# Four convolved feature chunks moved from the memory stage to the sample stage, and the decay sums of the SSD branch loaded from DRAM instead of multiplied on TensorE

## What is computed

```
h = _rmsnorm(x, norm_in_w)
u = h @ w_in
z_ssd, xbc, dt_raw, qkv, z_att, q_mem, z_mem, gate_raw = _split_in(u)
y_ssd = _ssd_branch(z_ssd, xbc, dt_raw, ...)    # conv(4)+SiLU on xbc, chunked scan, gated norm
outs, lses = dilated attention, 3 groups x 8 heads (sample queries read the caches)
y_att = merged outs * silu(z_att)
y_mem = _mem_attn(q_mem, mem_kv) * silu(z_mem)
merged = sum over branches of gate * (y_branch @ w_br)
y = _rmsnorm(x + merged @ w_out, norm_f_w)
```

```
acs = cumsum(dt * a_neg)                        # over the chunk's 128 tokens
lmat = exp(where(tril, acs[l] - acs[s], -inf))
y_diag = ((C B^T) * lmat) @ (x * dt)
```

## Time and profile before

| | us |
|---|---|
| median of 3 runs | 2171.91 |
| lowest and highest run | 2169.57, 2172.75 |
| profiled execution | 2172.42 |
| its span | 2170.6 |
| busy PE / DVE / ACT / POOL | 2029.3 / 990.8 / 755.5 / 237.5 |
| memory stage, 182 to 401 | 219.0, PE busy 219.0 |
| sample stage and set-up, 1092 to 1499 | 407.0, PE busy 377.3 |
| SSD core up to its seventh chunk, 1499 to 1764 | 265.0, PE busy 247.3 |

### The profile page before, as it was taken

One profiled execution on the slowest core, in us unless ns is written; L12 is line 12 of the kernel. 1 busy time (PEld: TensorE's weight loads), 2 busy tenths in 40 slices (PEclk: granted clock), 3 DMA queues, 4 the chain that ended last, 5 costly groups with the idle time before them and its releaser, 6 DMA issues.

```text
span 2170.6 us, 35280 instructions
## 1 busy us (share of the span) xinstructions
PE 2029.3 (93%) x14555; PEld 1929.4 (89%) x14555; DVE 990.8 (46%) x1948; ACT 755.5 (35%) x1635; POOL 237.5 (11%) x358
## 2 busy tenths in 40 slices
PE   5999999999989999999999789999999979969997
PEld 5899999999889999999999679759999969969997
DVE  5214676525454445343346871103444465454423
ACT  5223354223443323233645112305364553132202
POOL 1000112100001011112123000001111111100000
PEclk9999999999999999999999888999999989989998
DMA  6211233211112121212266665483333545554422
GB/s 211 88 42 60 80 91 90 82 46 51 37 32 66 38 66 47 77 63 67 87 196 193 209 209 161 165 297 110 108 117 101 163 145 179 166 183 136 137 82 104
DMA packets 166992, 248.76 MB, mean 115 GB/s; under 512 B 19701, under 2 KB 114613, under 8 KB 166805
## 3 DMA queue, kind: packets, MB, share of 16 engines
q1 hardware_dynamic: 144576, 179.51, 26.5%
q0 software_dynamic: 22256, 66.98, 9.1%
HBM read 179.74 MB, written 66.70 MB: 114 GB/s over the span
## 4 chain that ended last, share of the span: by engine, by line
PE 75%; DVE 9%; ACT 6%; DMA 5%; issue 4%; SPq 0%; DVEq 0%; POOL 0%; ACTq 0%; POOLq 0%
PE bank L2236 19%; PE bank L2237 18%; PE bank L2238 18%; PE bank L2432 2%; DMA acc<-acc_T 2%; PE bank L2407 2%; DVE w_lo L1698 2%; PE bank L2538 1%; PE bank L2390 1%; PE bank L2648 1%; PE bank L2368 1%; ACT soft L1512 1%; DVE softT L1950 1%; PE bank L2471 1%; ACT Lm L1625 1%
## 5 line engine op out<-in xcount | busy, mean ns | idle before, releaser
L2236 PE MATMUL bank<-w_hi,hT_hi 128*128 128x256 f32 (+1 forms) x1848 | 534.5, 289 | 3.4 <-DVE hT_lo L2106 3.4
L2237 PE MATMUL bank<-w_lo,hT_hi 128*128 128x256 f32 (+1 forms) x1848 | 522.7, 283 | 0.0
L2238 PE MATMUL bank<-w_hi,hT_lo 128*128 128x256 f32 (+1 forms) x1848 | 521.9, 282 | 0.0
L2236 PE MATMUL bank<-hT_hi,w_hi 128*128 128x352 f32 x1344 | 458.3, 341 | 6.3 <-DVE acc L2083 5.7
L2238 PE MATMUL bank<-hT_hi,w_lo 128*128 128x352 f32 x1344 | 444.7, 331 | 0.0
L2237 PE MATMUL bank<-hT_lo,w_hi 128*128 128x352 f32 x1344 | 444.4, 331 | 0.0
L2236 PEld LDWEIGHTS bank<-w_hi,hT_hi 128*128 128x128 f32 (+1 forms) x1848 | 347.5, 188 | 4.9 <-issue 3.6
L2238 PEld LDWEIGHTS bank<-w_hi,hT_lo 128*128 128x128 f32 (+1 forms) x1848 | 348.6, 189 | 0.6
L2237 PEld LDWEIGHTS bank<-w_lo,hT_hi 128*128 128x128 f32 (+1 forms) x1848 | 347.6, 188 | 0.7
L2236 PEld LDWEIGHTS bank<-hT_hi,w_hi 128*128 128x128 f32 x1344 | 263.6, 196 | 16.7 <-issue 7.5
L2237 PEld LDWEIGHTS bank<-hT_lo,w_hi 128*128 128x128 f32 x1344 | 264.1, 197 | 1.1
(11 more groups left out here) (417 smaller groups left out, 2993.9 us busy)
## 6 DMA issues: line engine op xcount, KB each, us to landing
w_raw<-in_w_in SPq DMA_DIRECT2D x96, 512.0 KB, 4.9
kvring<-in_cache_win_kv SPq DMA_DIRECT2D x120, 256.0 KB, 3.6
feat_T<-fstage POOLq DMA_DIRECT2D x40, 528.0 KB, 3.8
fstage<-feat_T SPq DMA_DIRECT2D x16, 528.0 KB, 4.4
xc<-feat_T SPq DMA_DIRECT2D x8, 1024.0 KB, 5.8
kvring<-in_cache_mem_kv SPq DMA_DIRECT2D x28, 256.0 KB, 3.8
o_rows<-obuf POOLq DMA_DIRECT2D x48, 132.0 KB, 2.0
mo<-o_rows SPq DMA_DIRECT2D x24, 264.0 KB, 3.9
```

The costliest lines, as they stand in the source:

```text
L2236: pe.matmul(out, xh(k), wh(k), start=(k == 0), stop=False)
L2237: pe.matmul(out, xh(k), wl(k), start=False, stop=False)
L2238: ins = pe.matmul(out, xl(k), wh(k), start=False, stop=(k == nk - 1))
```

## The change

**Part 1, the chunks.** `N_MEM_FILL` is 4: four of the eight convolved chunks move from the memory stage to the sample stage, behind the first two gate chunks, where they become chunks 38 to 41. The sample stage gets its fillers by part: 3 chunks beside the merges, 3.5 beside the 64 scored-on-DVE key sets, 1 beside the 24 turned ones, 1.5 beside the softmax, 3 beside the value sets; 12 where there were 9. A thirteenth follows beside the set-up, and the core holds 7 where it held 6. Value sets stand in groups of 4, not 8. The late convolved chunks all use `fraw_a`, are written in up to five pieces, and wait for the convolution of the feature before. SP waits for the store of the last convolved feature ahead of the first `xc`. A `low` never overtakes another.

**Part 2, the decay sums.** The 128 D products of the prompt's chunks (c below 8) are gone. One matmul in `ssd_dA` gives the running sums of all chunks and heads transposed (row = chunk and head, column = token); DVE copies them to `yraw`, SP writes them to DRAM (`sum_T`, 64 KB) and waits until they are there, then loads them back four rows at a time, broadcast over the 128 partitions (256 KB), into two slots `sums`: 32 loads, load i waiting for the relus of load i - 2. ACT's relu reads `sums` in SBUF in place of PSUM. The loads share the semaphores of the key and value loads.

```diff
-N_MEM_FILL, N_TAIL_FILL, N_SAMPLE_FILL = 8, 2, 9
+N_MEM_FILL, N_TAIL_FILL = 4, 2
+FILL_MERGE, FILL_KEYS, FILL_TURNED, FILL_SOFT, FILL_VALUES = 3, 3.5, 1, 1.5, 3
...
+    fill_src = conv[:N_MEM_FILL] + [("za", i, "w_in", C_ZATT + CW * i) for i in range(2)]
     fill_src += [("z", i, "w_in", C_Z + CW * i) for i in range(4)]
+    fill_src += gates[:2] + conv[N_MEM_FILL:] + gates[2:]
...
-    side += [sum(sval[i:i + 8], []) for i in range(0, len(sval), 8)]
-    sched += spread(side, steps)
+    parts.append(([sum(sval[i:i + 4], []) for i in range(0, len(sval), 4)], FILL_VALUES))
+    steps = gate_steps(round(sum(fill for _, fill in parts)))
...
+        while at < len(sched) and sched[at][0] == "low":
+            at += 1
...
+            def load_sums(i):
+
+                if i >= NSUM:
+                    sp.wait_ge(s_ddf, i - NSUM + 1)
+                sp.dma_start(sums[:, i % NSUM, :, :].rearrange("p h l -> p (h l)"),
+                             sumT[4 * i:4 * i + 4, :].rearrange("h l -> (h l)").partition_broadcast(P)).then_inc(sum_landed(i)[0], 16)
...
                     if c == 0:
                         late_free(sp)
+                        conv_stored(sp)
...
+                elif s[0] == "ssd_dA":
+                    late_free(sp)
+                    sp.wait_ge(s_s0, 4)
+                    first, count = value_sem(NRING), value_landed(len(values) - 1 - (len(values) - 1 - NRING) % NVAL)
+                    sp.dma_start(sumT, yraw[:, 0:P]).then_inc(first, 16)
+                    sp.wait_ge(first, count + 16)
+                    for i in range(NSUM):
+                        load_sums(i)
+                elif s[0] == "ssd" and s[2] in (1, 2) and s[1] < NB:
+                    for i in range(4 * s[1] + 2 * s[2] - 2 + NSUM, 4 * s[1] + 2 * s[2] + NSUM):
+                        if i < 4 * NB:
+                            load_sums(i)
...
-                            if c >= 2:
+                            if c > 2 * N_MEM_FILL:
+                                act.wait_ge(s_conv, c)
+                                act.wait_ge(s_tail[(c - 1) % 2], 32 * ((c + 1) // 2))
+                            elif c >= 2:
...
-                            act.wait_ge(s_dD, 4 * c + qq + 1)
+                            if c < NB:
+                                act.wait_ge(*sum_landed(4 * c + qq))
+                                later = sums[:, (4 * c + qq) % NSUM, :, :]
...
+                    dve.tensor_copy(yraw[:, 0:P], bank[7][:, P:2 * P])
...
+                    pe.matmul(bank[7][:, P:2 * P], dA[:, 0:P], table("upper"), start=True, stop=True)
...
-                    elif q in (1, 2):
-                        up = (table("upper") if c < NB else table("upper_s"))[0:m, 0:m]
+                    elif q in (1, 2) and c == NB:
+                        up = table("upper_s")[0:m, 0:m]
...
-                            pe.wait_ge(s_ddf, 4 * c + 8)
+                            pe.wait_ge(s_dxt, c + 2)
```

More of the change, by code:

```diff
@@ L272, in plan @@
     side += [[("sprep", 0)], [], [("sscore", 0)], []]
[L273 to L280 removed]
+    parts = [(side, FILL_MERGE)]
+    n_prod = 2 * TS * BS
+    for lo, hi, fill in ((0, n_prod, FILL_KEYS), (n_prod, len(sets) + 1, FILL_TURNED)):
+        parts.append(([[("skey", n) for n in range(i, min(i + 4, hi))] for i in range(lo, hi, 4)], fill))
+    parts.append(([[("ssoft", 0)], [], [], [("ssoft", 1)], [], [], [("ssoft", 2)], [], []], FILL_SOFT))
     sval = []
@@ L285, in plan @@
         sval[-1] += [("soT", y) for y in range(4) if part_end[y] + 5 == n]
-    side += [sum(sval[i:i + 8], []) for i in range(0, len(sval), 8)]
-    sched += spread(side, steps)
+    parts.append(([sum(sval[i:i + 4], []) for i in range(0, len(sval), 4)], FILL_VALUES))
+    steps = gate_steps(round(sum(fill for _, fill in parts)))
+    done, upto = 0, 0
+    for part, fill in parts:
+        upto += fill
+        last = round(len(steps) * upto / sum(f for _, f in parts))
+        sched += spread(part, steps[done:last])
+        done = last
     steps = gate_steps(1)
@@ L561, in build_program @@
         yraw = sb(area, "yraw", [P, TOK])
+        last = ExitStack()
+        sums = sb(last, "sums", [P, NSUM, 4, P])
+        last.close()
         yst2 = sb(area, "yst2", [P, KT8, NS])
@@ L919, in value_landed, with sum_landed @@
             return 16 * (n // NVAL + 1 + (key_loads((len(sets) + r) % NRING) if r < NRING else 0))
+        def sum_landed(i):
+            x = 3 + i % NSUM
+            return s_kv[x], 16 * (key_loads(x) + len(range((x - len(sets)) % NRING, len(values), NVAL)) + i // NSUM + 1)
         def probs_turned(eng, half):
@@ L1007, in wait_part1_stores, with conv_stored @@
                 eng.wait_ge(s_tail[i], 16 * 16)
+        def conv_stored(eng):
+            last = max(feat_no[x] for x in conv_no)
+            for i in range(2):
+                eng.wait_ge(s_fst[i], 16 * ((last + 2 - i) // 2))
+                eng.wait_ge(s_tail[i], 16 * 16)
         def gates_stored(eng):
```

38 lines of the change are left out of this document (20 added, 18 removed).

## The result

| | median us | lowest to highest | runs |
|---|---|---|---|
| before | 2172.33 | 2169.57 to 2176.25 | 4 |
| changed | 2217.88 | 2215.75 to 2219.12 | 4 |

A forecast was written before the change was run, and what follows sets the result against it. PE, busy 93% of the span, was taken as the bound. Memory stage -73, sample stage +19 and core +15 gave -39 us from 2172.4, so 2133 us; range 2107 to 2162, faster 0.87.

The forecast's parts named there:

- so -22: SSD core: removing the D products frees 16 x 1.87 = 30 us of PE, less the last two chunks, hence -22 us.
- 83 to 95: Value sets in the sample stage: PE work and transfers near equal, 83 to 95 us.
- Memory stage: Memory units: four chunks leave for -92.8 us, stalls give back 17 and lower clock 3, net -73 us.
- Merges, key sets, turned sets: Sample stage: merges 105 to 83 us, key sets 96 to 104, turned sets 63 to 74, softmax 31 to 42.
- Start: Start of the core: first transpose waits for `xc` behind the sums' write and loads, +13 us, between +4 and +20.
- Rival C: Value sets bound by transfers at 217 GB/s, 124 us in place of 95, whole 2162 us; chance 9%.
- go too: -5: SSD core: PE's waits for ACT's release of the D banks beside filler, 5.0 us, vanish: -5 us.
- Rival E: Core: D products were hidden in waits for DVE, removing them gains nothing, core +30 us, whole 2148; chance 8%.
- The split of chunk 50, +6: Core: this split waits on ACT for weights loaded after the previous `w_lo`, once on the path: +6 us, between 0 and 12.
- Rule on the relu: Core: skill's fixed costs make each SBUF relu 43 ns longer, 5.5 us of ACT, sum at most 1 us higher.
- rival D: Core: sums come late in every chunk, ACT waits some 3 us each, PE behind it: +18 us, 2151; chance 12%.

The follow-up runs named there:

- Part 2 alone: Only the loaded decay sums replacing D products, plan and fillers as before, against the kernel before: 2206.81 us, ratio 1.0174.
- part 1 alone: Only the chunks moved as in the change, D still multiplied on TensorE, no loads of sums, against the kernel before: 2195.57 us, ratio 1.0129.
- with the products back, unused: Kernel with only the loaded sums, but PE again makes the 128 D products, which nothing reads: 2192.44 us, ratio 1.0099 against the kernel before.

## Why the prediction was wrong

The forecast was 82 us off: -39 against a span 43 us longer. Two terms failed, the D products of the core ("so -22", and -5 with them) and the values ("83 to 95"); each of the others was within 9 us.

**Memory stage: right,** -71.5 for -73. PE stalls 13.5 us there, near the 17 taken; 3.9 of them are for DVE's `soft`, and the view names no releaser for most of the rest.

**Merges, key sets, turned sets:** -24.2 for -22, +16.6 for +8 and, with the softmax, +23.3 for +22. PE's waits for the key products fell from 19.7 to 5.0 us, as forecast, but PE had 106.9 us to do beside those sets where 96 were taken, and so was the bound. The clock rose to 0.98 there; beside the turned sets it fell, 0.86 to 0.73, where it was to rise, so that the right sum of that line is partly luck. A slip, too: the parts of the sample stage as listed add up to 414 to 426 us, not 406.

**Start: right in mechanism,** 17.8 for 13; the write alone held SP 5.6 us, where 2 were taken. Part 2 alone has it too, and moving `xc` ahead takes it away.

**"Values: 83 to 95": wrong,** it was 78.9 to 122.0. Two terms were mis-sized. The products of the value sets were set at about 10 us; four sets take 1.0 us of PE's time:

```profile
1411.54 0.63 PE L2597 MATMUL bank<-v_ring,pm_late 128*32 128x512 f32 x3
...
1412.54 0.43 PE L2295 MATMUL bank<-hT_hi,w_hi 128*128 128x352 f32 x1
```

88 sets are 22 us. With 18 thirds of 4.07 that is 95 and, with the reductions, 100: PE became the bound, and the ten added thirds (8 stood there before) cost their full price, 41 us. The other term is what comes on top of PE's work, 22 us where at most 6 were taken (95 less 88.5): 10.5 of it are waits, and the rest is work that takes longer behind them. (In the three other kernels with these steps it is 28 to 30.) Twelve value sets stand in a row between two thirds and wait for their loads, and a convolution stands on DVE in front of a reduction that PE waits for:

```profile
1336.76 1.92 PE L2597 MATMUL bank<-kvring,pm_late 128*32 128x512 f32 x2 [3.77 <-DMA kvring<-in_cache_win_kv]
...
1342.01 0.62 PE L2597 MATMUL bank<-kvring,pm_late 128*32 128x512 f32 x1 [1.47 <-DMA kvring<-in_cache_win_kv]
```

```profile
1382.46 1.89 PE L2603 MATMUL bank<-con,soft 128*128 128x16 f32 x8 [4.53 <-DVE soft L2067]
```

Rival C had a bound by transfers at 217 GB/s; it was PE, at 236.

**"D products: 16 x 1.87 = 30 us, so -22", and "go too: -5": wrong, and this is the largest.** The 1.87 us of the earlier trace rows is right. On top of part 1 the sums made the core stretch 4.6 us longer (294.1 to 298.7), where these terms say 27 shorter; on the kernel before, 12 longer. The two have different causes.

On the kernel before, the row of waits was read the wrong way round. PE waiting four times for ACT's Lm *with* the products in its queue says that ACT is nearly level with PE there. Take PE's work out of such a stretch and a wait takes its place, 4.0 us for 3.7 in SSD chunk 1. Rival E said this ("hidden in waits for DVE; the core costs +30") and was given 8%; by the prediction's own terms it costs +37 to +42. It fell short too, since PE works on at a lower clock behind such a wait (36.8 us for 33.4 of other work in SSD chunk 1): part 2 alone makes the core 12 us longer, not 0.

In the changed kernel, with seven thirds beside most SSD chunks, the saving does appear where nothing else is in the way: 3.0 us in SSD chunk 0 and 3.6 in SSD chunk 2 (the last two rows of the table of SSD chunks). SSD chunks 4 and 5 lose 6.6 and 6.9, and there theory S holds: ACT stands at a `w_hi` whose weights SP sends only behind the loads of sums. SP and ACT in SSD chunk 4, part 1 alone:

```profile
1661.34 0.98 SPq L1077 DMA_DIRECT2D w_raw<-in_w_in  x2
...
1682.77 1.90 ACT L1395 ACTIVATE w_hi<-w_raw 128x2048 fp32r<-128x2048 f32 x1
```

and in the changed kernel, with what PE then waits for:

```profile
1675.47 8.04 SPq L1069 DMA_DIRECT2D sums<-sum_T  x4
1683.55 0.98 SPq L1094 DMA_DIRECT2D w_raw<-in_w_in  x2
...
1690.88 1.91 ACT L1424 ACTIVATE w_hi<-w_raw 128x2048 fp32r<-128x2048 f32 x1 [7.05 <-DMA w_raw<-in_w_in]
...
1694.53 3.75 PE L2716 MATMUL bank<-state,xc 128*128 128x256 f32 x8 [6.14 <-ACT yst L1698]
```

The `w_lo` that frees the slot had ended at 1648.9, so it is SP that the weights waited for. In SSD chunk 5 the `w_hi` of a branch weight waits 7.1 us for the same reason, in front of two lots of relus, and PE waits 9.7 for Lm. These waits need SP's order and the plan together: with the same loads of sums and the fillers placed otherwise (235.8 us) there is none.

SSD chunk 7, beside which no filler chunk stands, went from 42.5 to 48.4, and the prediction had 0. It is not cover: with the products back, unused, it takes 48.8. There Y starts 18.3 us behind the first transpose, for 17.5 before, and then runs at a clock of 0.57, for 1.00 before. The product Y in SSD chunk 7, first in the kernel before, then with the products unused:

```profile
1777.78 3.68 PE L2648 MATMUL bank<-xdt,Lm 128*128 128x64 f32 x32
```

```profile
1794.52 6.35 PE L2685 MATMUL bank<-xdt,Lm 128*128 128x64 f32 x32 [2.15 <-DVE Lm L2170]
```

PE's work behind it runs at 0.76, for 0.92 before. So most of those 6 us is the lower clock behind the wait; why PE comes to wait in this place with loaded sums was not isolated.

**"The split of chunk 50, +6": right, but not once.** That wait is there, 6.75 us:

```profile
1647.74 3.47 PE L2716 MATMUL bank<-state,xc 128*128 128x256 f32 x8 [6.75 <-ACT yst L1698]
```

with ACT behind a load that SP sent when the `w_lo` before was made:

```profile
1644.71 1.91 ACT L1424 ACTIVATE w_hi<-w_raw 128x2048 fp32r<-128x2048 f32 x1 [7.63 <-DMA w_raw<-in_w_in]
```

It came again: two such waits for `yst`, 12.9 us, and ACT at `w_hi` for 42.5 us in five waits. The first is the plan's, as forecast: part 1 alone has it too, 5.7 us, and in the changed kernel the weights leave SP right behind the `w_lo` before. The second, in SSD chunk 4, is the one above, and comes of the loads of sums.

**Rule on the relu: agrees.** The forecast counted nothing for it. Four relus from SBUF take 1.26 to 1.28 us, from PSUM 1.12 to 1.14, 35 ns each:

```profile
L1683 ACT ACTIVATE Lm<-sums,sc 128x128 f32<-128x128 f32 x112 | 35.3, 389 | 0.9 <-DMA sums<-sum_T 0.9
```

The Trainium skill ("VectorE: DVE Perf Modes", the section on the trn2 errata) gives a ScalarE operation 224 cycles of fixed cost from SBUF and 172 from PSUM at 1.2 GHz, by which the difference is 43 ns, an estimate; the trace agrees nearly. The mean of the whole group went from 366 to 389. On a chain that has become the bound it does count, half a microsecond an SSD chunk. The last column of the row answers rival D as it was put: ACT waited 0.9 us for the sums in all. What came late behind the sums' queue were the weights.

## What to carry to other kernels

Before PE work is taken out of a stretch, lay out the other engines' chain between the same two points: if PE waits there at all, compare the two lengths (here a chain of 17.9 us beside 15.3 of PE work); where the chain is the longer, the work is cover, and taking it out pays only once filler moves in. Before loads that wait for something are put into an in-order queue, list what stands behind them: here the weights of the next chunk left SP some 21 us later. A "busy" PE with thin weight loads is not room for filler either: price its own products by their spacing (here 0.25 us a value set) before adding to them. And the gain of one part can hang on the order of another: the same two parts took 2217.9 us and, with the fillers and the first `xc` placed for the chain, 2151.8.
